# Adding the gathered row tiles on TensorE, and one VectorE operation for mean and norm weight, in the last stage of a hybrid decoder layer

## The reference, cut to what matters

```python
ffn = moe_ffn(x, ...)                       # routed experts + shared expert
x = layer_norm(ALPHA * x + ffn, ln2_g, ln2_b)

def layer_norm(x, g, b):
    mu = jnp.mean(xf, -1, keepdims=True)
    var = jnp.mean(jnp.square(xf - mu), -1, keepdims=True)
    return (xf - mu) * lax.rsqrt(var + LN_EPS) * g + b

routed = segment_sum(y_rows * row_gate[:, None], row_tok)[:n_tok]
shared = (silu(xt @ sh_wg) * (xt @ sh_wu)) @ sh_wd     # inside moe_ffn, for every token
```

## Time and profile before

| | us |
|---|---|
| median of 3 runs | 2111.48 |
| the runs | 2109.60 to 2112.53 |
| the profiled execution's own time | 2109.28 |
| its span in the trace | 2107.5 |
| TensorE busy | 2027.0 (96%) |
| VectorE busy | 1338.0 (63%) |
| ScalarE busy | 851.8 (40%) |
| GpSimd busy | 552.3 (26%) |

### The profile page before, as it was taken

One profiled execution on the slowest core, in us unless ns is written; L12 is line 12 of the kernel. 1 busy time (PEld: TensorE's weight loads), 2 busy tenths in 40 slices (PEclk: granted clock), 3 DMA queues, 4 the chain that ended last, 5 costly groups with the idle time before them and its releaser, 6 DMA issues. The chain is left out here.

```text
span 2107.5 us, 33125 instructions
## 1 busy us (share of the span) xinstructions
PE 2027.0 (96%) x9741; PEld 1438.3 (68%) x9742; DVE 1338.0 (63%) x2792; ACT 851.8 (40%) x1433; POOL 552.3 (26%) x358
## 2 busy tenths in 40 slices
PE   6999999999999999989999979999999999999995
PEld 5887787877778766668655546766666676667662
DVE  2595543444116777788456637777777777777756
ACT  2111221234112344430022246666666666666643
POOL 2343232333312211012100123323333332223324
PEclk8999999999999999999999999999999999999998
DMA  5113212221612210168660377899897989899857
GB/s 185 51 50 95 95 31 60 63 73 49 167 60 90 68 46 26 38 203 291 205 247 37 135 290 242 299 350 341 308 353 263 353 297 338 303 298 315 297 169 199
DMA packets 167729, 389.05 MB, mean 185 GB/s; under 512 B 26176, under 2 KB 98145, under 8 KB 142944
## 3 DMA queue, kind: packets, MB, share of 16 engines
q1 hardware_dynamic: 129680, 298.02, 38.8%
q0 software_dynamic: 28752, 73.18, 14.1%
q10 hardware_dynamic: 9216, 16.78, 2.1%
HBM read 337.04 MB, written 80.22 MB: 198 GB/s over the span
## 5 line engine op out<-in xcount | busy, mean ns | idle before, releaser
L627 PE MATMUL a_bank<-x_hi,w_hi 128*128 128x512 f32 x928 | 374.9, 404 | 8.9 <-DVE x_lo L1023 8.9
L627 PE MATMUL a_bank<-x_hi,w_lo 128*128 128x512 f32 x928 | 364.1, 392 | 0.0
L627 PE MATMUL a_bank<-x_lo,w_hi 128*128 128x512 f32 x928 | 363.4, 392 | 0.0
L1644 PE MATMUL e_bank<-w_gu,work 128*128 x616 | 277.1, 593 | 2.2 <-issue 1.4
L2159 DVE TENSOR_TENSOR d_lo<-w_d,d_hi 128x1024 fp32r<-128x1024 f32 x152 | 179.8, 1224 | 60.2 <-ACT d_hi L1928 60.2
L565 POOL CAST w_hi<-w_raw 128x1024 fp32r<-128x1024 f32 x56 | 64.8, 1157 | 574.6 <-PE a_bank L627 574.6
L627 PEld LDWEIGHTS a_bank<-x_hi,w_hi 128*128 128x128 f32 x928 | 175.5, 189 | 50.6 <-issue 13.5
L627 PEld LDWEIGHTS a_bank<-x_hi,w_lo 128*128 128x128 f32 x928 | 175.3, 189 | 38.3
L627 PEld LDWEIGHTS a_bank<-x_lo,w_hi 128*128 128x128 f32 x928 | 175.8, 189 | 34.3 <-issue 0.5
L1644 PEld LDWEIGHTS e_bank<-w_gu,work 128*128 128x128 f32 x616 | 111.8, 191 | 113.4 <-issue 113.4
L1840 ACT ACTIVATE u_hi<-w_gu 128x1024 fp32r x150 | 159.0, 1061 | 1.9 <-POOL work L1533 1.7
(11 more groups left out here) (361 smaller groups left out, 3795.1 us busy)
## 6 DMA issues: line engine op xcount, KB each, us to landing
w_d<-in_moe_wd SPq DMA_DIRECT2D x64, 1024.0 KB, 12.8
w_gu<-in_moe_wg SPq DMA_DIRECT2D x64, 1024.0 KB, 7.9
w_gu<-in_moe_wu SPq DMA_DIRECT2D x64, 1024.0 KB, 11.3
w_raw<-in_w_in SPq DMA_DIRECT2D x54, 512.0 KB, 3.8
gates<-gate_out ACTq DMA_DIRECT2D x64, 256.0 KB, 2.0
g_sb<-gates SPq DMA_DIRECT2D x16, 1024.0 KB, 5.4
acc_odd<-zero POOLq DMA_DIRECT2D x9, 512.0 KB, 14.0
work<-in_w_out SPq DMA_DIRECT2D x4, 1024.0 KB, 8.4
```

What stands on the lines that cost most here:

```text
L627: ins = pe.matmul(bank[h][:, :], w[:, c % 2, k, :], x[:, k, cols], start=(k == 0 and j == 0), stop=(k == KD - 1 and j == 2))
L1644: ins = pe.matmul(out, x_gt[:, s, k, :], w_gu[:, bass.ds(e & 3, 1), :, k, :].rearrange('p a m f -> p (a m) f'), start=k == 0, stop=k == KD ...
```

## The change

TensorE gets four additions, `tail_add(t)` for t = 4 to 7: two products of the identity with the two halves of `rows2[:, t]`, accumulated onto the down product in the same banks. Each waits for `odd_in[t]`, and it is now `tail_add` that raises `s_down`. VectorE has no addition any more: for t >= 4 it reads statistics and values straight from the banks, and frees them by `gained` instead of `s_y`, behind its last read.

The norm is computed in another order. VectorE subtracts the mean and multiplies by g2 in one operation (lines 2252 and 2256), ScalarE's `normal` then only multiplies by the scale (behind `gained`), and GpSimd's addition of b2 waits for `normed`. `scales` is one reciprocal. Tile 7 is finished by VectorE in one operation a half instead of two (2263), without ScalarE. `tail_hidden(6)` stands behind tile 0's norm instead of ahead of it.

```diff
@@ gpsimd
             for t in range(NT - 1):
-                pool.wait_ge(gained, t + 1)
+                pool.wait_ge(normed, t + 1)
@@ tensor, tail_down
                 if t >= NU + 2:
-                    pe.wait_ge(s_y, t - 1)
+                    pe.wait_ge(gained, t - 1)
...
+            def tail_add(t):
+
+                pe.wait_ge(odd_in[t], 16)
+                for h in range(2):
+                    ins = pe.matmul(bank[2 + 2 * (t % 2) + h][:, :], ident, rows2[:, t, h * HALF:(h + 1) * HALF],
+                                    start=False, stop=True)
                 ins.then_inc(s_down, 1)
...
             tail_turn(5)
+            tail_add(4)
             tail_down(5)
             shared_up(7)
             tail_turn(6)
+            tail_add(5)
             tail_down(6)
+            tail_add(6)
             tail_turn(7)
             tail_down(7)
+            tail_add(7)
@@ scalar
             def normal(t):
                 act.wait_ge(scale_done, t + 1)
-                act.activation(rows2[:, t, :], rows2[:, t, :], ACT.Identity, scale=scale[:, t:t + 1],
-                               bias=shift[:, t:t + 1]).then_inc(normed, 1)
+                act.wait_ge(gained, t + 1)
+                act.activation(rows2[:, t, :], rows2[:, t, :], ACT.Copy, scale=scale[:, t:t + 1]).then_inc(normed, 1)
...
-            normal(NT - 1)
@@ vector
-                dve.wait_ge(odd_in[t], 16)
-                if t >= NU:
+                halves = [slice(h * HALF, (h + 1) * HALF) for h in range(2)]
+                if t < NU:
+                    dve.wait_ge(odd_in[t], 16)
+                    src = [rows2[:, t, cols] for cols in halves]
+                else:
                     dve.wait_ge(s_down, t + 1)
-                    for h in range(2):
-                        cols = slice(h * HALF, (h + 1) * HALF)
-                        ins = dve.tensor_tensor(rows2[:, t, cols], rows2[:, t, cols], bank[2 + 2 * s + h][:, :], ALU.add)
-                    ins.then_inc(s_y, 1)
-                    dve.wait_ge(s_y, t + 1)
+                    src = [bank[2 + 2 * s + h][:, :] for h in range(2)]
                 for h in range(2):
-                    ins = dve.bn_stats(stats[:, s, h, :], rows2[:, t, h * HALF:(h + 1) * HALF])
+                    ins = dve.bn_stats(stats[:, s, h, :], src[h])
                 X(ins)
                 dve.bn_aggr(mv[:, s, :], stats[:, s, :, :]).then_inc(mv_done2, 1)
                 if t:
                     scales(t - 1)
-                if t >= 2:
-                    gain(t - 2)
+                dve.wait_ge(mv_done2, t + 1)
+                if t < NU:
+                    dve.scalar_tensor_tensor(rows2[:, t, :], rows2[:, t, :], mv[:, s, 0:1], g2, ALU.subtract, ALU.mult
+                                             ).then_inc(gained, 1)
+                else:
+                    for h in range(2):
+                        ins = dve.scalar_tensor_tensor(rows2[:, t, halves[h]], src[h], mv[:, s, 0:1], g2[:, halves[h]],
+                                                       ALU.subtract, ALU.mult)
+                    ins.then_inc(gained, 1)
             scales(NT - 1)
...
+            for cols in halves:
+                dve.scalar_tensor_tensor(rows2[:, NT - 1, cols], rows2[:, NT - 1, cols], scale[:, NT - 1:NT], b2[:, cols],
+                                         ALU.mult, ALU.add).then_inc(last_done, 1)
```

More of the change, by code:

```diff
@@ L1726, in tail_down @@
                 if t >= NU + 2:
-                    pe.wait_ge(s_y, t - 1)
+                    pe.wait_ge(gained, t - 1)
                 for h in range(2):
                     for j in range(2):
-                        ins = pe.matmul(bank[2 + 2 * (t % 2) + h][:, :], tail_t[:, t % 2, j, :],
-                                        tail_d[:, j, h * HALF:(h + 1) * HALF], start=j == 0, stop=j == 1)
+                        pe.matmul(bank[2 + 2 * (t % 2) + h][:, :], tail_t[:, t % 2, j, :],
+                                  tail_d[:, j, h * HALF:(h + 1) * HALF], start=j == 0, stop=False)
+            def tail_add(t):
[3 more added lines that the diff above has]
+                                    start=False, stop=True)
                 ins.then_inc(s_down, 1)
@@ L2212, in _ @@
             tail_hidden(5)
-            dve.wait_ge(s_ht, NU + 1)
-            tail_hidden(6)
             dve.wait_ge(ln_in2, 32)
             def scales(t):
-                s = t % 2
                 dve.wait_ge(sd_done2, t + 1)
[L2221 to L2227, removed]
+                dve.reciprocal(scale[:, t:t + 1], sd[:, t % 2:t % 2 + 1]).then_inc(scale_done, 1)
             for t in range(NT):
                 s = t % 2
+                if t == 1:
+                    dve.wait_ge(s_ht, NU + 1)
+                    tail_hidden(6)
                 if t == 5:
@@ L2246, in _ @@
                     scales(t - 1)
-                if t >= 2:
-                    gain(t - 2)
-            scales(NT - 1)
[L2250 to L2255, removed]
+                dve.wait_ge(mv_done2, t + 1)
[7 more added lines that the diff above has]
+                    ins.then_inc(gained, 1)
+            scales(NT - 1)
+            dve.wait_ge(scale_done, NT)
+            dve.wait_ge(gained, NT)
+            for cols in halves:
+                dve.scalar_tensor_tensor(rows2[:, NT - 1, cols], rows2[:, NT - 1, cols], scale[:, NT - 1:NT], b2[:, cols],
+                                         ALU.mult, ALU.add).then_inc(last_done, 1)
 def program(nc, d, consts, c_at, consts_moe, e_at, out):
```

## The result

| | before | changed |
|---|---|---|
| median, us | 2111.48 (5 runs) | 2121.85 (5 runs, 2120.60 to 2122.76) |
| profiled execution, own time | 2109.28 | 2122.42 |
| its span | 2107.5 | 2120.6 |
| SP's first load of the rows | 2048.03 | 2049.32 |
| from there to the end of the span | 59.5 | 71.3 |

The changed kernel is slower by 10.4 us: the ratio is 1.0053, with a 95% interval of 1.0041 to 1.0064, which is 8.7 to 13.5 us. (A ratio here is estimated from all the runs of both kernels, so it need not be the quotient of the two medians.) The prediction was 2124.0 with a range of 2118.5 to 2127.5.

A forecast was written before the change was run, and what follows sets the result against it. The last stage's chain was taken as bound by TensorE to the end of up 7, then ScalarE, from 2087.9 us VectorE. 10.0 - 2.6 + 2.6 + 2.5 = +12.5 us on 2111.48 gave 2124.0, range 2118.5 to 2127.5.

The forecast's parts named there:

- The wait: TensorE at the first addition, behind turn 5: stands still for tile 4's DMA landing from 2066.4 to 2075.2, 8.8 us.
- Up to U: TensorE from tile 4's landing through first addition, down 5 and up 7: 12.3 us at full clock, ending 10.0 later.
- U: Moment when TensorE ends up 7, the shared up product of tile 7: 2077.54 us before, predicted 2087.5 at full clock.
- Behind U: Tail from the end of up 7 to the span's end: 27.4 us instead of 29.96, 2.6 less, before clock loss.
- The second pause: TensorE ahead of the last down, waiting for VectorE's combined operation of tile 5 behind tile 4's reciprocal: 3.6 us.
- the second fall of the clock: TensorE's clock dropping to 1.2 GHz at the pause ahead of the last down: +2.5 us, the least certain term.
- Rival 1: Only TensorE's first pause, for tile 4's landing, costs clock: +10.0, 2121.5 us; chance 0.22.
- rival 4: Worse: tile 4 lands a microsecond or two later, longer low clock, VectorE ahead of GpSimd: up to +16, 2127.5; chance 0.12.
- Rival 2: No visible clock loss on TensorE behind either pause: +7.4, 2118.9 us; chance 0.08.
- Rival 3: TensorE doesn't wait, as tile 4 is there when turn 5 is done: -1.4, 2110.0 us; chance 0.10.
- VectorE as the bound (5): VectorE's work per late tile would exceed TensorE's: 2.9 us against 5.2 and more; given no chance of its own.
- VectorE's saving: VectorE's dropped additions and shift and scale copy: counted in the tail's number, or bringing nothing ahead of up 7's end.

The follow-up runs named there:

- e1: Changed kernel, but tile 4's identity products on TensorE read a long-landed tile and VectorE waits for the DMA instead; 2109.99 us, ratio 0.9997 to the kernel before.
- e5: Changed kernel plus ten extra identity products on TensorE between turn 5 and the first addition, filling the DMA wait; 2119.33 us, ratio 1.0035 to the kernel before.
- e4: Changed kernel with tile 4's reciprocal on VectorE moved behind tile 5's combined operation; 2117.24 us, ratio 1.0034 to the kernel before.
- e9: Changed kernel unaltered, measured and profiled a second time; 2119.66 us, ratio 1.0036 to the kernel before.
- e6: Changed kernel with TensorE's addition of tile 4 moved behind turn 6, so behind down 5 and up 7; 2112.05 us, ratio 0.9999 to the kernel before.
- e2: Changed kernel's norm alone, with TensorE as in the kernel before and VectorE adding the rows; 2106.91 us, ratio 0.9985 to the kernel before.
- e8: Changed kernel, but VectorE adds tiles 4 and 5, TensorE only 6 and 7, reciprocals behind combined operations, VectorE finishes tile 6; 2102.20 us, ratio 0.9952 to before.
- e10: Changed kernel unaltered, one third execution; 2181.88 us, with its last stage beginning some 60 us late and 69.3 us long.

## Why the prediction was right

**The wait.** The prediction read from the earlier trace rows that TensorE would stand still for 8.8 us. It was 8.7. e1 shows the causal side: without this wait, and with all new operations in place, the loss is gone.

**Up to U.** The landing came 27.0 us behind the start of the stage, where the sum had 27.2. From the restart to U it had 12.3 us and 2.6 for the clock, 14.9; measured 2091.00 - 2076.35 = 14.65. e5 confirms the split: 12.3 and 2.35.

**Behind U.** It had 27.4 us and 2.5 for the clock, 29.9; measured 2120.6 - 2091.0 = 29.6. The second pause was to be 3.6 us and was 3.7, for the reason given (e4 takes it away by the order on VectorE alone). The clock's share was 6.64 - 3.70 = 2.9 instead of 2.5. The end was as described in its outline: VectorE's first last half and GpSimd's addition of tile 6 meet (in this timeline GpSimd's starts at 2113.83), VectorE's takes 2.78 us where its second takes 0.67, and the stores leave together. In its size two errors cancel. The last work ends at 2117.4 us, U + 26.4, where the sum had about U + 25.6 with the clock; from there to the end of the span it takes 3.2 us and not 4.3 (3.8 and 0.5).

```profile
2113.83 2.34 POOL L1570 TENSOR_TENSOR x<-x,w_gu 128x1024 f32<-128x1024 f32 x1 [4.96 <-ACT x L1976]
```

**The sum.** +12.5 was predicted, the stage is 11.8 longer, the medians differ by 10.4 (interval 8.7 to 13.5), and by 8.6 in e9 (4.6 to 10.8). The median forecast, 2124.0, is 2.15 us above what was measured. The step that was too sure is the second fall of the clock, which the forecast took as coming, because its pause of 3.6 us lay between two lengths behind which the clock had fallen. Its own rows 5 held a case that doesn't fit such a reading: the low stretch from 33.97 us on stands behind a pause of only 1.73 us, ahead of which TensorE was busy for less than half of each microsecond. In the windows (last numbers: granted clock, DMA share, GB/s) the fall lies in that pause:

```profile
33.00:34.00 1.00, 0.03 (x1) 0.69 1.09 330
```

That the second fall was there in the profile is in part luck. It came in full in the three profiles of the changed kernel (2.9, 2.6 and 2.6 us of the last down), with 1.7 us in e1, and not at all in e5 and e6, behind the same pause. If some of the unprofiled executions are without it, their median lies below the profiled stage. That would account for the difference, and so would the scatter of the medians, whose interval holds both 11.8 and 12.5 for the first pair. No run shows the clocks of unprofiled executions stretch by stretch, so it stays open.

**The rivals.** Rival 1, only the first fall (2121.5), is closer to the median (by 0.35 us) than the forecast; three profiles of the changed kernel out of three have both falls, and so speak for the forecast's picture. Rival 2 falls with them. Of rival 4 the late landing didn't come (13.9 us instead of 14.8). Rival 3, no wait, falls with the first row of the waits. VectorE as the bound (5) was rightly given nothing: it waits for TensorE for 7.2 us in all.

**VectorE's saving.** The prediction said that what VectorE saves is in the number for the tail or lies ahead of U, where VectorE waits anyway. In the changed kernel that is so. e2 shows what it is worth where VectorE is the bound, as it was before: 3.9 us by the median. One part of it is in no duration that the prediction lists. Behind U the kernel before had the shift of tile 6, one element per row and 0.16 us elsewhere, beside an addition of GpSimd, and it took 2.33 us on the chain that ended last:

```profile
2096.44 2.34 POOL L1570 TENSOR_TENSOR x<-x,w_gu 128x1024 f32<-128x1024 f32 x1 [1.82 <-DVE x L2227]
2096.47 2.33 DVE L2222 SCALAR_TENSOR_TENSOR ln_shift<-ln_mv,ln_sd 128x1 f32<-128x1 f32 x1
```

The new form has no shift. At the full clock the tail behind U is 29.6 - 2.9 = 26.7 us, 3.3 shorter than before's 29.96.

## What to carry to other kernels

A late landing costs nothing as long as its reader comes later. Moving a read to an engine that reaches it earlier turns the same landing into a wait of everything queued behind, so read the landing column before moving a read, not only the durations. And when a buffer is freed by a later operation than before, look at what stands between in that engine's queue: here one reciprocal of 0.1 us carried a wait of 6 us for another engine's square root. Taking over only the reads whose data have landed, with the queues ordered so that TensorE waits for no square root, and with the end given to VectorE, e8 came out 10 us below the kernel before where the change lay 10 above it. Last, look for small operations beside a GpSimd addition: here one of 0.16 us took 2.33 there, on the path.

## What the runs showed of the hardware

The fall of TensorE's clock is not told by the length of the pause ahead of it. It came behind a pause of 1.9 us in e2 (1.4 us after the restart) and not behind the same pause in the kernel before; in the pause of 1.73 us ahead of 33.97 us in the kernel before; behind 3.7 us in the changed kernel and e1 and not in e5 and e6. Behind the long pauses, 7.7 to 8.9 us, it came each time that TensorE stood idle, and not in e5, where the wait was filled. Ahead of the last down it cost 1.7 to 2.9 us when it came. In the last stage it was up again 3.3 us (e10, first pause) to 6.0 us (changed kernel, second pause) behind the restart.

VectorE's combined operations at 1024 columns took 1.28 us alone and 2.17 in e2 where GpSimd's addition ran beside them, both inputs being in SBUF; those with one input in PSUM took 1.41 for two halves in the changed kernel, beside GpSimd's additions (at 2103.78 us) and away from them (at 2081.74) alike. The Trainium skill (SBUF — State Buffer, section "Who interferes with whom") has an exclusive lock between VectorE operations with two SBUF inputs and GpSimd's reads, and this trace agrees: VectorE's first last half, 2.78 us from 2113.93 on, ends 0.54 us behind GpSimd's addition, which started 0.10 us ahead of it.

In the changed kernel the lengthened combined operations (2.15 and 1.81 us) lay ahead of U, where VectorE had time, and cost nothing; the lengthened last half lay on the path and cost 2.1 us.
